# A hybrid layer's mixer in a new order: token-major keys and values, top-k under the value projection, the output product in three parts

## The reference, cut to what matters

```
h = rmsnorm(x, g_mix) @ w_in                      # 2048 -> z 1024, xbc 1536, dt 16, q 1024, k 512, v 512, qi 1024, ki 64, wi 16
xbc = silu(causal_dwconv(xbc) + bias)             # 4 taps; gives xs (1024), B and C (2 groups x 128)
dt = softplus(dt + dt_bias);  a = -exp(a_log)
y = ssd_chunked(xs, dt, a, B, C) + d_skip * xs    # 16 heads of 64
y = rmsnorm_per_group(y * silu(z)) * g_ssd        # 2 groups of 512
q, k, ki = rmsnorm per head (gains g_q, g_k, g_kidx)
score[t, s] = sum_h relu(qi_h[t] . ki[s]) * wi_h[t]    # 16 index heads
keep the 64 best admissible keys of each query; softmax attention over them, 8 heads, 4 key-value heads
x = x + concat(y, attention) @ w_out
x = x + square(relu(rmsnorm(x) @ w_up)) @ w_down       # 2048 -> 8192 -> 2048
```

## Time and profile before

| | us |
|---|---|
| median of 3 runs | 2867.19 (2867.06 to 2867.64) |
| the profiled execution, its own time | 2869.21 |
| its span, first to last instruction | 2867.5 |
| TensorE / VectorE / ScalarE / GpSimd busy | 2754.4 / 1701.8 / 1319.4 / 45.4 |

### The profile page before, as it was taken

One profiled execution on the slowest core, in us unless ns is written; L12 is line 12 of the kernel. 1 busy time (PEld: TensorE's weight loads), 2 busy tenths in 40 slices (PEclk: granted clock), 3 DMA queues, 4 the chain that ended last, 5 costly groups with the idle time before them and its releaser, 6 DMA issues.

```text
span 2867.5 us, 44523 instructions
## 1 busy us (share of the span) xinstructions
PE 2754.4 (96%) x15472; PEld 2405.7 (84%) x15472; DVE 1701.8 (59%) x2352; ACT 1319.4 (46%) x1781; POOL 45.4 (2%) x92
## 2 busy tenths in 40 slices
PE   7999999999999999999999979877699999999999
PEld 6999997888888888888888879877588888888887
DVE  5666666555555655656555665855656556565564
ACT  5454454444445544444444544345545444344443
POOL 1000000000000000000000000100000000000000
PEclk9999999999999999999999989998899999999999
DMA  6555555666665555555555534532255555555555
GB/s 215 182 174 170 192 182 175 203 201 195 202 208 179 191 194 188 189 192 185 195 185 189 176 111 143 159 103 88 74 190 183 191 191 185 196 183 191 190 189 170
DMA packets 139814, 509.01 MB, mean 178 GB/s; under 512 B 15895, under 2 KB 16215, under 8 KB 139176
## 3 DMA queue, kind: packets, MB, share of 16 engines
q1 hardware_dynamic: 135736, 494.36, 52.7%
q0 software_dynamic: 2720, 10.68, 1.2%
q10 hardware_dynamic: 1232, 2.16, 0.2%
HBM read 502.88 MB, written 4.19 MB: 177 GB/s over the span
## 4 chain that ended last, share of the span: by engine, by line
PE 87%; DVE 7%; ACT 3%; issue 2%; DVEq 0%; DMA 0%; ACTq 0%; SPq 0%
PE acc L1562 17%; PE acc L1563 8%; PE acc L1547 5%; PE acc L1549 5%; PE acc L1548 5%; PE pT L1580 4%; PE pS L1580 4%; PE pS L1579 4%; PE pT L1579 4%; PE pS L1578 4%; PE pT L1578 4%; PE acc L1578 3%; PE acc L1580 3%; PE acc L1579 3%; PE pO L1579 2%
## 5 line engine op out<-in xcount | busy, mean ns | idle before, releaser
L976 DVE TENSOR_TENSOR wlo<-raw,whi 128x1024 fp32r<-128x1024 f32 x938 | 1147.8, 1225 | 890.4 <-ACT whi L551 889.0
L551 ACT ACTIVATE whi<-raw 128x1024 fp32r<-128x1024 f32 x938 | 991.2, 1058 | 1014.2 <-PE pT L1580 335.5
L1562 PE MATMUL acc<-a_w,whi 128*128 128x512 f32 x2048 | 723.0, 398 | 0.0
L1563 PE MATMUL acc<-a_w,wlo 128*128 128x256 f32 x2048 | 574.2, 280 | 0.0
L1547 PE MATMUL acc<-a_w,whi 128*128 128x256 f32 x1744 | 517.7, 297 | 26.8 <-DVE a_w L989 19.6
L1548 PE MATMUL acc<-a_w,whi 128*128 128x256 f32 x1744 | 504.4, 289 | 0.0
L1549 PE MATMUL acc<-a_w,wlo 128*128 128x256 f32 x1744 | 504.0, 289 | 0.0
L1562 PEld LDWEIGHTS acc<-a_w,whi 128*128 128x128 f32 x2048 | 384.7, 188 | 95.8 <-DVE a_w L1010 0.7
L1563 PEld LDWEIGHTS acc<-a_w,wlo 128*128 128x128 f32 x2048 | 386.6, 189 | 0.3
L1547 PEld LDWEIGHTS acc<-a_w,whi 128*128 128x128 f32 x1744 | 346.7, 199 | 34.3 <-DVE a_w L989 19.8
L1548 PEld LDWEIGHTS acc<-a_w,whi 128*128 128x128 f32 x1744 | 346.5, 199 | 2.7 <-issue 1.9
(11 more groups left out here) (345 smaller groups left out, 3434.6 us busy)
## 6 DMA issues: line engine op xcount, KB each, us to landing
raw<-stream SPq DMA_DIRECT2D x938, 512.0 KB, 3.3
gbias<-gateb POOLq DMA_DIRECT2D x12, 256.0 KB, 4.1
xF<-x SPq DMA_DIRECT2D x2, 1024.0 KB, 6.7
bias_scratch<-brow POOLq DMA_DIRECT2D x8, 256.0 KB, 3.8
X<-x_rows POOLq DMA_DIRECT2D x1, 2048.0 KB, 9.3
out<-X ACTq DMA_DIRECT2D x8, 256.0 KB, 4.5
bias<-bias_scratch POOLq DMA_DIRECT2D x8, 128.0 KB, 4.0
wg<-gates POOLq DMA_DIRECT2D x8, 128.0 KB, 3.0
```

The costliest lines, as they stand in the source:

```text
L551: A(whi[:, slot, :], raw[:, slot, :], ACT.Copy).then_inc(s.hi_done, 1)
L976: TT(wlo[:, slot, :], raw[:, slot, :], whi[:, slot, :].bitcast(F32), SUB).then_inc(s.lo_done, 1)
L1562: MM(ps, wh, wide[:, k0 + k, :], start=start and k == 0, stop=False, skip_group_check=True)
L1563: last = MM(ps[:, 0:T], wl, wide[:, k0 + k, 0:T], start=False, stop=not start and k == KC - 1, skip_group_check=True)
```

## The change

The first layer stays as it is. In the second layer's mixer the number of chunks stays 122, their order and their side work change:

1. k (8 chunks) and v (8 chunks) are made token-major with `chunk_tok`. Their norm factors are two columns per head on the partitions of the tokens; k is then scaled and transposed, v is only scaled.
2. All reciprocal square roots of the mixer and of both MLPs are made on VectorE from small tiles: a bit operation for a start value and three Newton steps (`rsqrt_small`). ScalarE's Ln and its `preload_act_table_set` go from these places.
3. The sums of squares of q and y come from one-column products (`q_stat`, `y_stat`); the factor of q goes into the logits (`attn_logits2`), that of y into the evacuation of the output product.
4. dt is handled on 128 partitions with 32 columns, its running sum by a product with a triangular matrix (`upto`).
5. Order: k, small, qi, v, four rounds (B or C unit, q unit), four rounds (xs, q), four rounds (xs, z), 4 units of z, and the output product. Top-k begins at the last two chunks of v and continues through the B/C rounds. One attention head goes with each xs round, the convolution's first tap moves to ScalarE, and the SSD's eight pairs are spread over the last 4 units of z and the first 16 chunks of the output product.
6. The output product has three parts: attention half for the four column groups, then for each column group the first and the second 512 rows of y. That is 12 evacuations of two halves in place of 4.
7. The mixer is written out with no hardware loop, and GpSimd stages nothing.

The diff, cut:

```diff
-L2_UNITS = 1 + 4 + 4 + 8 + 12 + 16
+L2_CHUNKS = 90
+L2_EVACS = 4 + 8 + 8
...
+            def rsqrt_small(v, y, w, dst):
+                step(TS(y.bitcast(I32), v.bitcast(I32), 1, 0x3fffffff, ALU.logical_shift_right, ALU.bitwise_xor))
+                step(TS(y, y, RSQRT_SCALE, None, MUL))
+                for k in range(3):
+                    step(TT(w, y, y, MUL))
+                    step(STT(w, w, -0.5, v, MUL, MUL))
+                    step(STT(dst if k == 2 else y, w, 1.5, y, ADD, MUL))
...
             # ScalarE
+            square_x(G_MLP1 + 15, NG - 1, 8, 1, s.x2_done)
+            l2_prep(1)
+            l2_prep(2)
             norm_hi(2, NG - 1, "g_mix2")
...
+            def attention_round(c, h, n, k):
+                l2_prep(c)
...
+                attn_exp(At(8 + h))
+                l2_prep(c + 1)
+                conv_first(n, k)
+                l2_prep(c + 2)
+                attn_pt(At(8 + h))
+                conv_tanh(n)
...
             # VectorE
             times_final(NG - 1)
+            l2_prep(0)
+            total_squares(24, 2, 3)
+            rsqrt_tok(ss[:, 0, :], r1T)
+            step(TT(rrT, ss[:, 1, :], r1T, MUL))
+            step(TT(rrT, rrT, r1T, MUL))
+            rsqrt_tok(rrT, r2T)
...
+            l2_prep(1)
...
+            l2_prep(2)
             turned_lo(2, NG - 1, "g_mix2")
...
+            for r in range(2):
+                l2_prep(32 + r)
+                top(r)
+            for p in range(4):
+                c = 34 + 4 * p
+                l2_prep(c)
+                if p == 0:
+                    dve.wait_ge(s.cleared, 1)
+                    top(2)
+                conv_in(p, 9 + 2 * p, c + 1)
+                l2_prep(c + 1)
+                conv_taps(p, 8 + p)
+                l2_prep(c + 2)
+                if p < 3:
+                    top(3 + 2 * p)
+                l2_prep(c + 3)
+                conv_out(p, bc[:, p, :])
+                if p < 2:
+                    top(4 + 2 * p)
...
+            for p in range(8):
+                c, n = 50 + 4 * p, 4 + p
+                if p % 4 == 0:
+                    q_factors(p // 4)
+                attn_logits2(p)
+                l2_prep(c)
+                if p >= 5:
+                    z_out(p - 5)
+                conv_in(n, 17 + 2 * p, c + 1)
+                attn_norm(At(8 + p))
+                l2_prep(c + 1)
+                conv_taps(n, p)
+                if p:
+                    xtok_scale(p - 1)
+                l2_prep(c + 2)
+                if p >= 4:
+                    z_in(p - 4, 18 + 2 * p, c + 3)
+                l2_prep(c + 3)
+                conv_out(n, xs[:, p, :])
+                attn_lo(At(8 + p), b_lo[:, 8 + p, :], b_hi[:, 8 + p, :])
...
             # TensorE
+            for j in range(8):
+                if j == 3:
+                    turn_x(G_MLP1 + 15, NG - 1, s.x2_done)
+                pe.wait_ge(s.a_ready, 32 + 2 * j + 2)
+                chunk_tok(At(B_L2 + j), At(G_K), (pO, pG), a_w, 2 * j, j == 0, j == 7)
...
+            for p in range(8):
+                c, u = 50 + 4 * p, 17 + 2 * p
+                half_unit(c, u, 0)
...
+                attn_scores(At(8 + p), q_f[:, p, :], kN[:, p // 2, :])
+                half_unit(c + 1, u, 1)
+                if p:
+                    xs_turn(p - 1)
+                half_unit(c + 2, u + 1, 0)
+                attn_transpose(At(8 + p))
+                if 1 <= p < 4:
+                    q_stat(3 + p)
+                half_unit(c + 3, u + 1, 1)
...
+                attn_pv(At(8 + p), vtk[:, 0, P * (p // 2):P * (p // 2) + P], vtk[:, 1, P * (p // 2):P * (p // 2) + P])
+            for p in range(4):
+                c, u = 82 + 2 * p, 33 + p
+                half_unit(c, u, 0)
+                if p == 0:
+                    xs_turn(7)
+                ssd_bc(p)
+                half_unit(c + 1, u, 1)
+                if p:
+                    ssd_y(p - 1)
+                if p >= 2:
+                    y_stat(p - 2)
...
             for n in range(NG):
-                i = At(G_OUT2 + n)
-                for j in range(8):
-                    if n == 0 and j >= 4:
-                        pe.wait_ge(s.gn_ready, 2 * j - 6)
-                    chunk_tok(At(B_OUT2 + 8 * n + j), i, tbanks(i), b_w, (2 * j + 8) % 16, j == 0, j == 7)
+                for g in range(2):
+                    c, i = 106 + 4 * n + 2 * g, G_OUT2 + 4 + 2 * n + g
+                    for k in range(2):
+                        if n == 0:
+                            pe.wait_ge(s.gn_ready, 4 * g + 2 * k + 2)
+                        out_chunk(c + k, i, 4 * g + 2 * k, k == 0, k == 1)
```

More of the change, by code:

```diff
@@ L499, in _ @@
[L499 to L513, removed]
@@ L529, in _ @@
[L529 to L535, removed]
+            pool.wait_ge(s.mix_ready, 8)
+            for k in range(2):
+                last = nc.gpsimd.memset(cb[k], 0.0)
+            last.then_inc(s.cleared, 1)
         @block.scalar
@@ L746, in _, with mlp @@
                             mix_hi(At(3))
-            def mlp(b, a, i0, layer, stage, norm, gain, before):
+            def mlp(b, a, i0, layer, stage, gain, before):
                 for g in range(FF_GROUPS):
@@ L790, in mlp, with l2_prep @@
                         down(n, g == FF_GROUPS - 1)
[L792 to L798, removed]
-            c = At(B_L2)
+            mlp(B_MLP1, A_MLP1, G_MLP1, 0, 1, "g_mlp1", G_OUT1 + NG - 1)
+            def l2_prep(c):
+                prep(At(B_L2 + c))
@@ L877, in xs_copy @@
[L877 to L888 removed]
+            for c in range(3, 7):
+                l2_prep(c)
@@ L1287, in times_final, with mlp @@
                     TT(xg, xg, fgB[:, COLS * n:COLS * n + COLS], MUL).then_inc(s.x2_done, 1)
-            def mlp(b, a, i0, layer, stage, norm, gain):
+            def mlp(b, a, i0, layer, stage, gain):
                 for g in range(FF_GROUPS):
@@ L1565, in chunk_wide, with half_unit, chunk_tok @@
                 last.then_inc(s.mm_done, 1)
-            def chunk_tok(c, i, banks, src, k0, first, last):
+            def half_unit(c, u, half):
+                if half == 0 and u >= 2:
+                    scaled = unit_scaled(u - 2)
+                    n = sum(unit_scaled(k) == scaled for k in range(u - 1))
+                    pe.wait_ge(s.evacuated if scaled else s.unit_copied, A_L2 + n if scaled else n)
+                c, ps = At(B_L2 + c), unit_bank(u)
+                slot = c.mod(NSLOT)
+                pe.wait_ge(s.lo_done, c.value(1))
+                for k in range(KC):
+                    wh, wl = (w[:, slot, P * k:P * k + P] for w in (whi, wlo))
+                    hi, lo = a_w[:, 8 * half + k, 0:T], a_w[:, 8 * half + k, T:2 * T]
+                    MM(ps[:, 0:T], wh, hi, start=half == 0 and k == 0, stop=False)
+                    MM(ps[:, 0:T], wh, lo, start=False, stop=False)
+                    last = MM(ps[:, 0:T], wl, hi, start=False, stop=half == 1 and k == KC - 1)
+                last.then_inc(s.mm_done, 1)
+            def chunk_tok(c, i, banks, src, k0, first, last, units=None):
                 slot = c.mod(NSLOT)
@@ L1745, in _ @@
                             turn_x(G_OUT1 + n - 1, n - 1)
-            def unit(c, a):
-                chunk(c, a, a_w, 0, stop=False)
-                chunk(c.plus(1), a, a_w, 8, start=False)
             def mlp(b, a, i0, layer, stage, before):
-                pe.wait_ge(s.t_evac, 2 * before + 2 * NG - 2)
+                pe.wait_ge(s.t_evac, 2 * before)
                 for g in range(FF_GROUPS):
@@ L1850, in xs_transpose, with q_stat @@
[L1850 to L1862 removed]
+            def q_stat(p):
+                pe.wait_ge(s.q_sq, p + 1)
+                if p == 4:
+                    pe.wait_ge(s.q_factor, 1)
+                for h in range(2):
+                    last = MM(pN[:, 2 * p + h:2 * p + h + 1], sqq[:, P * h:P * h + P], ones[:, 0:1], start=True, stop=True)
+                last.then_inc(s.q_stat, 1)
```

1102 lines of the change are left out of this document (601 added, 501 removed).

## The result

| us | before | after |
|---|---|---|
| median | 2867.41 (4 runs, 2867.06 to 2867.96) | 2752.89 (4 runs, 2750.96 to 2754.61) |
| span of the profiled execution | 2867.5 | 2750.6 |

The ratio (time after over time before) is 0.960, 95% interval 0.9584 to 0.9617: 114.5 us less, for 114 predicted.

A forecast was written before the change was run, and what follows sets the result against it. Mixer bound by TensorE, with 118.7 of 517.1 us lost to waits and low clock. Own work 397.3 plus 6 losses gives 403.3, or -113.8: 2867.2 to 2753.4, say 2753; range 2741 to 2793.

The forecast's parts named there:

- TensorE's own work is almost unchanged; the gain comes out of waits and the low clock: Mixer: own work 398.4 us before, 397.3 after; 118.7 lost before to waits and low clock; 6 taken for remaining losses.
- The waits come from chains within a round: Mixer before: TensorE's waits (23.6 us on transposed probabilities, 16.0 on scores, 9.2 on a square) follow from cross-engine chains.
- Table loads: Mixer's ScalarE: about one load remains, and 31 us of ScalarE go with the waits around them.
- Attention rounds: Eight rounds: TensorE 13.4 us each, VectorE about 11.4, ScalarE 7.3; probabilities at 7.9, transposes at 9.5; loss 0 to 2.
- q_factors rounds, the cover: Two attention rounds with 2.8 us of q_factors: probabilities about 10.2 for 9.9 to 11.3; ordinary rounds have 1.6 us spare.
- The start: Mixer's start: 34 VectorE steps, 6.8 us; last columns ready 0.9 us before chunk 6; loss 0 to 2, 1 taken.
- Top-k: "about 6 us of delay cost nothing": B/C rounds: VectorE backlog under 3 us, top-k round about 1.6; a prep can come about 6 us late for free.
- Output: Output product: twelve evacuations cost VectorE 11.8 us more; the old tail and GpSimd's copies go; cost 0 to 2.
- rival 1: Attention rounds: the waits return because in-order queues lag and the 1.6 us are not there; 2793 us, chance 0.12.
- VectorE sets the pace (2): Attention rounds: VectorE work 15% above count makes a round 14.9 us; +12, 2765; chance 0.12 together with rival 3.
- rival 3: Exp and tanh load tables each time; z rounds lose about 1 us each; 2760; chance 0.12 together with rival 2.
- the low clock (5): Mixer: low clock stays while work is thin, chunks 5.1 us; 2919 if all 74 channel-major ones run so; chance 0.04.

The follow-up runs named there:

- runs 8 and 9: Kernel after, with two and four extra 128x512 VectorE operations ahead of the logits in each of the eight attention rounds: 2754.17 and 2757.19 us.
- run 7: Kernel after, with a table load forced ahead of each attention round's exponentials and a second at the convolution's tanh, 16 loads: 2754.11 us.
- run 10: Kernel after, with eight extra 128x512 VectorE operations ahead of the logits in each of the eight attention rounds: 2790.46 us.
- run 11: Kernel after, with the last six rounds of top-k in one lump at chunk 34: 2761.23 us, ratio 0.9624.
- run 12: Kernel after, with 20 more small VectorE steps in the start chain ahead of the input's last columns: 2756.21 us.
- run 2: Kernel before, with Exp in place of Tanh in z's gate in the q/z rounds: 2867.08 us, ratio 0.9996.

## Why the prediction was right

- **TensorE's own work is almost unchanged; the gain comes out of waits and the low clock.** Right. The mixer is 399.2 us for 403.3, 4.1 less. That the median still meets the prediction within 1 us is in part luck: the profiled execution of before took 1.8 us more than the median, the mixer begins 0.9 us later, and these make up for most of the 4.1. The one-column products were priced at 8.0 and cost 5.8 to 7.5 (16 pairs of 0.36 to 0.47); what is left over the own work is 2.4 to 4.1 us for the 6 taken.
- **The waits come from chains within a round.** Right, and now with sizes: taking the norm of q out of before gave 49.3 us, top-k 9.1, the shorter softplus 4.2; putting four SSD pairs back ahead of the output costs 28.9 us of stage time. Together about 91 of 114.5. They were tried one by one, and the last is an edit of after whose order is not that of before, so the sum is no proof that they add up. The rest (the norms of k and ki, the stop at v, GpSimd's copies, the hardware loop) was not tried by itself.
- **Table loads.** Partly wrong in what it suggests. None is left (one was predicted). But of the 31 us of ScalarE it is the eight before q's Ln that stood in a chain, worth 11 to 13 us; the eight at tanh cost nothing that shows. The Trainium skill ("ScalarE: Activation LUTs", section "What ACT_TABLE_LOAD costs") gives 1.38 us of drain beside the load. The run with forced loads shows a switch with work on both sides (ScalarE's timeline):

```profile
1833.21 0.47 ACT L605 ACTIVATE PTs<-pT 128x384 f32<-128x384 f32 x1
1833.71 1.28 ACT L838 ACT_TABLE_LOAD   x1
1835.00 0.42 ACT L838 ACTIVATE cth<-cv 128x256 f32<-128x256 f32 x1
```

  It takes 1.3 us from the end of the copy to the start of the tanh; the drain isn't seen.
- **Attention rounds.** Right: 53.87 us for the last four, 13.5 each, for 13.4 predicted; probabilities at 7.8 for 7.9; ScalarE 7.2 a round for 7.3. VectorE was counted too high: 10.4 for 11.4, and 74% of the mixer for 79%. I added durations, but its records overlap: a prep of 1.23 us at 1829.69 is followed at 1830.83. Measured durations add up to 11.2 a round, so the overlap is most of the difference.
- **q_factors rounds, the cover.** Loss 0 measured, 0 to 2 allowed. The cover of an ordinary round was undersized (1.6 for about 3).
- **The start.** Loss 0 for 1; the chain behaves as counted (0.20 a step), and k and small take 28.85 us. The 0.9 us to spare were right in size (the last columns at 1653.0, chunk 6 at 1653.8) but wrong in what they guard: chunk 6 needs only columns 12 and 13, ready at 1652.2, and a `wlo` is late sooner.
- **Top-k: "about 6 us of delay cost nothing".** This step failed, at no price to the sum, since no such delay occurs. It looked at preps alone. An evacuation has its due time too: the bank of the first B unit is free at 1753.6 (below) and wanted at 1757.0, where chunk 38 starts, 3.4 us later. The lump passed that first. A round of top-k was also counted a little short at 1.6 us: it takes 1.70 here, from 1751.50 to 1753.20.

```profile
1753.20 0.42 DVE L1421 TENSOR_TENSOR cb<-acc,rB 128x256 f32<-128x256 f32 x1
```

- **Output.** Right: 101.85 us, with clock 1.00 and no gap.
- **Rivals.** None came. That waits return (rival 1) needs some 3 us more in each round, by the runs 8 and 9; that VectorE sets the pace (2) isn't reached even with 5.8 us more; no table load is left, so rival 3 has nothing to act on, and its price stays open, since it had its 7 us in the z rounds and run 7 forced loads in the attention rounds alone (0.9 us, where the rival too saw next to none); the low clock (5) needs stops of the kind in runs 10 and 11.

## What to carry to other kernels

Before asking how long an engine is busy, ask in how many hand-overs a result comes back to the engine that sets the end, and move work until each such way is shorter than the work beside it; here this gave 4% with TensorE's own work almost unchanged. Work taken off an engine pays only if it stood in such a way: eight table loads were worth about 11 to 13 us, eight equal ones nothing that shows. When counting how much delay is free, go through everything queued behind it, banks that wait for an evacuation first, and take the nearest due time.

## What the runs showed of the hardware

- A stop of TensorE can cost more than its length. Behind the 5.3 us stop, 5.5 us ran at clock 0.55 (run 11); with stops of 2.6 to 5.5 us in eight rounds 25.7 us of stops made 37.3 us of growth (run 10); a single stop of 1.7 us left the clock of its window at 1.00 (run 12).
- A forced table set is loaded each time, also where the set is already in (run 2: 1.283 us each, 15 in the mixer, and no other load stands between the eight of the q/z rounds).
- An activation with two operands by pointer is longer: the convolution's first tap takes 0.587 us, a tanh of the same size with none 0.408 (ScalarE's groups in the mixer after):

```profile
L828 ACT ACTIVATE cv<-cb,convh 128x256 f32<-128x256 f32 x12 | 7.0, 587 | 1.1 <-DVE cb L1421 1.1
...
L836 ACT ACTIVATE cth<-cv 128x256 f32<-128x256 f32 x12 | 4.9, 408 | 1.5 <-DVE cv L1429 1.5
```

  The Trainium skill ("ScalarE: Activation LUTs", section "What ACT_TABLE_LOAD costs") gives 93 ns for each such operand; the trace agrees, 0.179 for two.
